# Two-layer hybrid trunk on one core: three instead of four of the plain gate and up tiles in halves of the tokens

## The reference

```
for l in range(2):
    h = rms_norm(x, pre_mix_g[l])
    z = h @ w_in[l]                       # gMLP u, gMLP v, q, k, v
    y_a = spatial gating of gelu(u), gelu(v)
    y_b = differential attention, 4 heads, block-causal
    x = x + rms_norm(concat(y_a, y_b) @ w_out[l], post_mix_g[l])

    h = rms_norm(x, pre_ffn_g[l])
    gate, up = split(h @ w_gate_up[l])    # 1024 -> 2 x 2816
    x = x + rms_norm((silu(gate) * up) @ w_down[l], post_ffn_g[l])
```

## Time and profile before

| | |
|---|---|
| median of three runs | 1087.66 us |
| profiled execution: its own time | 1087.47 us |
| its span, first to last instruction | 1085.3 us |
| TensorE matmuls busy | 1077.2 us (99%), 6840 matmuls |
| VectorE busy | 601.7 us (55%) |
| ScalarE busy | 585.8 us (54%) |
| GpSimd busy | 573.9 us (53%) |
| mean granted TensorE clock | 0.999 |

### The profile page before, as it was taken

One profiled execution on the slowest core, in us unless ns is written; L12 is line 12 of the kernel. 1 busy time (PEld: TensorE's weight loads), 2 busy tenths in 40 slices (PEclk: granted clock), 3 DMA queues, 4 the chain that ended last, 5 costly groups with the idle time before them and its releaser, 6 DMA issues.

```text
span 1085.3 us, 17599 instructions
## 1 busy us (share of the span) xinstructions
PE 1077.2 (99%) x6840; PEld 968.0 (89%) x6840; DVE 601.7 (55%) x1011; ACT 585.8 (54%) x1143; POOL 573.9 (53%) x450
## 2 busy tenths in 40 slices
PE   8999999999999999999999999999999999999997
PEld 7878888999999999888888888889999999988886
DVE  4374544888888884010345646458888888820103
ACT  6767784666555554221457578656565555531212
POOL 3533264567666665544444234645766666655440
PEclk9999999999999999999999999999999999999999
DMA  8423212424433434522243222242443343263212
GB/s 281 137 65 92 78 56 82 155 79 117 117 97 100 117 100 169 178 97 97 86 143 102 78 79 78 68 125 81 118 117 97 98 117 103 93 215 121 96 55 77
DMA packets 144791, 118.33 MB, mean 109 GB/s; under 512 B 3754, under 2 KB 120004, under 8 KB 144708
## 3 DMA queue, kind: packets, MB, share of 16 engines
q1 hardware_dynamic: 144692, 117.20, 34.3%
q10 hardware_dynamic: 16, 0.00, 0.0%
HBM read 110.90 MB, written 6.29 MB: 108 GB/s over the span
## 4 chain that ended last, share of the span: by engine, by line
PE 99%; ACT 0%; DMA 0%; DVE 0%; issue 0%; DVEq 0%; ACTq 0%
PE banks L604 30%; PE banks L606 30%; PE banks L605 30%; PE banks L669 2%; PE banks L697 2%; PE banks L613 1%; PE banks L682 1%; PE banks L873 1%; PE banks L707 1%; DMA x_rows<-in_x_dram 0%; PE banks L714 0%; ACT junk L1086 0%; PE banks L964 0%; PE banks L958 0%; DVE scratch L1502 0%
## 5 line engine op out<-in xcount | busy, mean ns | idle before, releaser
L535 POOL TENSOR_TENSOR w_lo<-raw,w_hi 128x512 fp32r<-128x512 f32 x204 | 259.6, 1296 | 299.1 <-ACT w_hi L1078 299.1
L553 POOL TENSOR_TENSOR w_lo<-raw,w_hi 128x512 fp32r<-128x512 f32 x200 | 260.8, 1315 | 141.4 <-ACT w_hi L1147 137.0
L604 PE MATMUL banks<-xg_hi,w_hi 128*128 128x256 f32 (+1 forms) x896 | 276.3, 308 | 0.0
L606 PE MATMUL banks<-xg_lo,w_hi 128*128 128x256 f32 (+1 forms) x896 | 274.2, 306 | 0.0
L605 PE MATMUL banks<-xg_hi,w_lo 128*128 128x256 f32 (+1 forms) x896 | 274.0, 306 | 0.0
L1078 ACT ACTIVATE w_hi<-raw 128x1024 fp32r<-128x1024 f32 x102 | 107.0, 1060 | 161.4 <-PE banks L606 146.9
L1147 ACT ACTIVATE w_hi<-raw 128x512 fp32r<-128x512 f32 x200 | 125.1, 630 | 114.8 <-DVE raw L1795 61.1
L606 PEld LDWEIGHTS banks<-xg_lo,w_hi 128*128 128x128 f32 x896 | 171.2, 191 | 7.8
L604 PEld LDWEIGHTS banks<-xg_hi,w_hi 128*128 128x128 f32 x896 | 171.2, 191 | 7.7
L605 PEld LDWEIGHTS banks<-xg_hi,w_lo 128*128 128x128 f32 x896 | 171.3, 191 | 6.9
L604 PE MATMUL banks<-w_hi,hid_hi 128*128 128x512 f32 x352 | 137.2, 390 | 0.0
(11 more groups left out here) (182 smaller groups left out, 1878.5 us busy)
## 6 DMA issues: line engine op xcount, KB each, us to landing
raw<-in_w_gate_up_dram SPq DMA_DIRECT2D x88, 512.0 KB, 4.1
raw<-in_w_down_dram SPq DMA_DIRECT2D x44, 512.0 KB, 3.5
raw<-in_w_in_dram SPq DMA_DIRECT2D x40, 512.0 KB, 3.8
raw<-in_w_out_dram SPq DMA_DIRECT2D x16, 512.0 KB, 3.5
x_spill<-x_rows SPq DMA_DIRECT2D x8, 512.0 KB, 4.3
x_rows<-x_spill SPq DMA_DIRECT2D x8, 512.0 KB, 4.7
x_rows<-in_x_dram SPq DMA_DIRECT2D x4, 512.0 KB, 7.4
out_dram<-x_rows SPq DMA_DIRECT2D x8, 256.0 KB, 2.0
```

The lines of the kernel that those rows point to most:

```text
L535: last = tt(lo[:, piece], raw_half(l, c, h)[:, piece], hi[:, piece].bitcast(F32), ALU.subtract)
L553: tt(lo, full, hi.bitcast(F32), ALU.subtract).then_inc(w_ready, 1)
L604: mm(o, stat[0], mov[0], start=first, stop=False)
L606: return mm(o, stat[0], mov[1], start=False, stop=last)
```

## The change

Row 3 is turned one half tile sooner, before `gate_up(1, 0, left)` and not behind it. The left half of tile (1, 1) is no longer made by itself; the tile is made over all 512 tokens, as the last of the plain ones. In the diff `2 * F0 - 1` is 3, so the loop makes the right halves of (0, 0), (0, 1) and (1, 0).

```
                 pe.wait_ge(xg_ready, 8 * group + 4)
+
                 gate_up(l, 0, 0, left, False)
                 turn_rows(group, 2)
                 gate_up(l, 0, 1, left, False)
+                turn_rows(group, 3)
                 gate_up(l, 1, 0, left, False)
-                turn_rows(group, 3)
-                gate_up(l, 1, 1, left, False)
                 pe.wait_ge(xg_ready, 8 * group + 8)
-                for f in range(F0):
-                    gate_up(l, f, 0, right)
-                    gate_up(l, f, 1, right)
+                for n in range(2 * F0 - 1):
+                    gate_up(l, n // 2, n % 2, right)
+                gate_up(l, 1, 1)
                 for f in range(F0, FT):
                     gate_up_blocks(l, f)
```

## The result

The changed kernel takes 1090.42 us (median of 11 runs, 1090.21 to 1090.55) against 1087.63 us before (11 runs, 1087.57 to 1087.85): 2.79 us longer, a quarter of a per cent, a ratio of 1.0025 with a 95% interval of 1.0018 to 1.0033. The prediction was 1090.5, range 1089.6 to 1091.8, slower.

A forecast was written before the change was run, and what follows sets the result against it. TensorE's matmuls were taken as the bound; per layer a 1.78 us stop less 0.32 us saved gives 1.46, together 2.92 us, summing to 1090.6 us. It said 1090.5, range 1089.6 to 1091.8.

The forecast's parts named there:

- What bounds: Whole kernel: TensorE's matmuls, busy 1077.2 of 1085.3 us; each matmul removed is time gained, each wait added time lost.
- its second rival: In that POOL run's own forecast: the later low parts make a wait of their own, over 1088; no chance given.
- The saving: Tile (1, 1): 24 matmuls of 512 columns replace 48 of 256, saving 0.32 us per layer, 0.64 us in all.
- The stop at the turn: Row 3's earlier turn: TensorE waits on DVE's normalising of the row, costing 1.78 us per layer.
- The lower bound that I gave with 0.40: Row 3's turn: last four transposes take 0.40 instead of 0.52 us, so the stop costs at least 1.66 us.
- The waits behind it: After the turn, at `xg_ready`: the turned row is ready with 1.0 us of cover, costed at nothing.
- That DVE might be done sooner: Row 3's normalising runs unstretched and ends 0.86 us earlier: net 0.60 us per layer, 1088.8; chance 0.08.
- The second wait: `xg_ready` or a sum of blocks is late beyond its cover, say 0.5 us per layer: 1091.5; chance 0.05.
- the clock: The stall at the turn drops TensorE to 1.2 GHz, up to 2.9 us more per layer: 1096; chance 0.02.
- the missing wait: At row 3's turn TensorE does not wait at all, only the saving is left: 1087.0; chance 0.04.

The follow-up runs named there:

- the first POOL order: Kernel before: POOL's low part of tile (1, 0) follows row 2's normalising; row 1's sums, then tile (1, 1)'s low part, follow row 3's; 1091.45 us.
- The split of the u tiles: Kernel before, all four u tiles of each layer made in halves, 48 matmuls of 256 columns for 24 of 512; 1090.22 us.
- POOL's order on the changed kernel: Changed kernel, POOL's low part of tile (1, 0) after row 2's normalising, row 1's sums and tile (1, 1)'s low part after row 3's; 1087.29 us.

## Why the prediction was right

- **What bounds.** Right. What the passage gains or loses shows one for one in the time (table above). Eight of nine runs came within 0.25 us of the time that was expected of them, and the ninth, the first POOL order, took the wait that its second rival named.
- **The saving.** Predicted 0.32 us a layer. The merged tile took 224.70 - 219.23 = 5.47 us instead of 5.44, since its first matmuls are a little further apart after narrow ones, so 0.29 us here. The split of the u tiles measured 0.32.
- **The stop at the turn.** Predicted 1.78 us a layer, measured 1.67. DVE's finish (207.17 here, 207.00 without the 0.17 us by which this execution is late, 207.02 predicted) and the 0.05 us behind it held. What was off is the price of the last four transposes: 0.52 us at the kernel's start, 0.42 us here (207.22 to 207.64). The lower bound that I gave with 0.40 was nearer. 0.11 us a layer too much, 0.03 too little elsewhere: a sum of 2.92 where the passages show 2.74. That the stated 1090.5 lies within 0.1 us of the measured 1090.42 is in part rounding: the sum itself gave 1090.6.
- **The waits behind it.** Right: 1.0 us of cover predicted at `xg_ready`, 210.59 - 209.56 = 1.03 us measured, and no wait in the block stage.
- **The rivals.** That DVE might be done sooner was priced at 1088.8 with 0.86 us off; in the changed kernel it did not happen. The run that made it happen shows that the mechanism is real and larger than priced (1087.29), because POOL, with the sums for row 1, stretched row 2's pair too, and so held row 3's residual up: 3.08 us in the changed kernel's trace, 1.41 with POOL out of the way. The rival had looked at the low parts and row 3 alone. The second wait, the clock and the missing wait did not show.
- **Not foreseen.** The prediction treated the early turn as the mistake and the merge as the gain. The runs show that with the late turn the merge costs 3 us as well. What the change spends is 2.9 us of work that TensorE had while row 3 was made ready, and with the other engines' order as it was, none of the three places tried for the turn makes up for it.

## What to carry to other kernels

On an engine that never starves, price a merge of two half jobs twice: what the merged instructions save (here 13 ns each), and what the half that was done early had been hiding (here 2.9 us of cover, where 1.2 us were to spare). Moving the step that feeds the wait decides at which semaphore the stop appears and can shorten it (from 2.8 to 1.6 us in all here), but it does not bring the cover back. Before giving such an edit up, look at what sets the late engine's finish: here another engine's unurgent work ran beside it, and putting that off turned 2.8 us lost into 0.4 us won, and into 0.6 with the turn moved to suit.

## What the runs showed of the hardware

The DVE operation here that reads two tensors from SBUF is stretched while POOL reads and writes SBUF: `scratch<-x_rows,rs_x,gpre` on 512 elements takes 0.74 us alone, 1.60 us beside POOL's low parts until 205.80, and a pair of them 3.08 us beside POOL's sums for row 1 in the passage above, against 1.41 us with POOL held off. Operations that take one of their tensors from a PSUM bank are not stretched: `x_rows<-banks,rs_y,x_rows` keeps 0.75 us with POOL busy beside it, as here in the changed kernel, where POOL runs from 200.48 to 205.96, and all 16 of this line in that kernel lie between 0.749 and 0.753 us. POOL is held up as well: its two sums of row 1 take 3.01 us beside the pair (197.51 to 200.52), and 2.55 us beside DVE's `xg_lo<-banks,xg_hi` in the run with POOL's order on the changed kernel (from 205.51).

```profile
197.99 3.08 DVE L1502 SCALAR_TENSOR_TENSOR scratch<-x_rows,rs_x,gpre 128x512 f32<-128x512 f32 x2
...
201.78 0.75 DVE L1536 SCALAR_TENSOR_TENSOR x_rows<-banks,rs_y,x_rows 128x512 f32<-128x512 f32 x1
```

```profile
200.48 5.48 POOL L535 TENSOR_TENSOR w_lo<-raw,w_hi 128x512 fp32r<-128x512 f32 x4
```

The Trainium skill (GPSIMD Engine Reference, section "Specifications") names contention with DVE instructions that have two SBUF inputs; the trace agrees, and gives the size.

TensorE's granted clock stayed at its upper level of 2.4 GHz through a stop of 1.67 us amid dense work: 1.00 in both passages' windows above.
